# Expert matrix w2 loaded as two adjacent rows per partition instead of two rows 128 apart

## The chip, the cores and the metric

The kernel runs on one core of one Trainium2 chip, as a single launch. The metric is the device time in microseconds (us), read as the median over runs. Weights start in the chip's main memory (HBM) and reach the core's on-chip memory of 128 partitions (SBUF) by DMA; TensorE (PE) multiplies, and VectorE (DVE), ScalarE (ACT) and GpSimd (POOL) do the elementwise work. SyncE (SP) issues nearly all transfers here. Every core has 16 DMA engines, over which each transfer is spread.

## The reference

The program is one inference step of a hybrid decoder layer in float32: 256 prompt tokens and 8 sample tokens of width 1024 (and 16 meta tokens in front of the prompt) pass a normalisation, an input projection, a short convolution and a gated recurrence, an output projection, and then a mixture of 32 experts, 4 of which each token uses. The change lies in the experts:

```python
def _moe(x, router_w, router_b, w1, b1, w2, b2):
    logits = x.astype(jnp.float32) @ router_w.astype(jnp.float32) + router_b.astype(jnp.float32)
    top_logits, top_idx = lax.top_k(logits, TOP_K)
    gates = jax.nn.softmax(top_logits, axis=-1)
    combine = jnp.einsum('tk,tke->te', gates,
                         jax.nn.one_hot(top_idx, N_EXPERTS, dtype=jnp.float32)).astype(x.dtype)
    out = jnp.zeros_like(x)
    for e in range(N_EXPERTS):
        a = x @ w1[e] + b1[e]                      # w1[e]: 1024 x 2048
        glu = jnp.minimum(a[:, ::2], SWIGLU_LIMIT)
        lin = jnp.clip(a[:, 1::2], -SWIGLU_LIMIT, SWIGLU_LIMIT)
        act = glu * jax.nn.sigmoid(SWIGLU_ALPHA * glu) * (lin + 1)
        out = out + combine[:, e:e + 1] * (act @ w2[e] + b2[e])   # w2[e]: 1024 x 1024
    return out
```

All 32 experts' weights are read, 12 MiB each in float32, 384 MiB together.

## The kernel before

**Two parts.** The first 240 us or so hold the token mixers, the routing and the gathering of tokens. From there on the kernel runs over the experts in 16 pairs. The function `pair` on PE takes two experts at once: each expert has room for 64 tokens (`CAP`), and its two halves of the PE array compute expert 0 and expert 1 of the pair side by side.

**What one pair does on PE, in program order.** The bias (L1316); 128 matmuls with w1 (L1354), which walk over the 8 row tiles `t` of w1, for both experts; the gather of the next pair's tokens (L1307, 72 short matmuls); adding back the rows of the pair before (L1324, 6 products); three transposes of the gather matrix (L1373); eight transposes of the activations (L1381); and 64 matmuls with w2 (L1394), again over 8 row tiles. Between L1354 and L1381 DVE and ACT apply the gated activation into `lin`, a tile of 128 partitions (64 tokens of each expert) by 1024 columns, one column for each row of w2. A transpose of `lin` puts 128 of its columns on the partitions, ACT copies it from PSUM to `actT3` (L666), and `actT3[:, t]` is then the stationary operand of the products with row tile `t` of w2.

**The ring.** `ring` has 16 slots of one load each, 1 MiB (128 partitions of 8 KB). A pair needs 24 loads (`LOADS`): j = 0 to 15 are the row tiles of w1, alternating between the two experts, and j = 16 to 23 are w2, where one load holds two row tiles (`t` and `t + 1`) of one expert. SP issues the loads in this order with `load` (the first pair) and `load_pair` (the rest), w1 at L357 and w2 at L359. Before each load it waits for `w_used`, which PE raises when it has finished with a slot. PE in turn waits for a load's own semaphore (`landed`). So nothing but free slots and the transfers themselves set when a load starts, and the SP queue holds nothing but these loads in the expert stage.

**The views that say which rows go where.** One w1 load gives partition p a whole row of 2048 numbers, one run of 8 KB. One w2 load covers 256 rows of 1024 numbers; `w2_v` says that partition p takes row p and row 128 + p of them (`a` = 0 and 1), two runs of 4 KB that lie 512 KB apart in HBM:

```python
w1_v = expert_w1[0].rearrange("e (t p) n -> e t p n", p=P)
w2_v = expert_w2[0].rearrange("e (r a p) n -> e r p a n", a=2, p=P)
```

The rows that are multiplied together must be the same on both sides: with `w2_v` as above, row tile `t` is rows 128t to 128t + 127, and the transpose at L1381 reads columns 128t to 128t + 127 of `lin`.

Of the kernel before, what the change touches and what calls it, by code (L numbers as in the profile page):

```python
# [25 lines left out]
P = 128  # L26
# [31 lines left out]
def build_step(nc, x_prompt, x_sample, state_conv, state_rec, meta_tokens, norm_mix, w_in, conv_w,  # L58
# [4 lines left out]
    with ctx:  # L63
# [11 lines left out]
        def take(n):  # L75
            a = top[0]
            top[0] += n
            assert top[0] <= ARENA, top[0]
            return mem[:, a:a + n]


        ident = take(P)
# [32 lines left out]
        def from_(ap, n, at=0):  # L115

            return mem[:, ap.offset + at:ap.offset + at + n]
# [81 lines left out]
        glu, sig, lin = [from_(vtok, D, D * n) for n in range(3)]  # L199
# [91 lines left out]
        w_sb = {g: cut(slots(a), 512) for g, a in {FX: 6, IV: 14, QG: 10, OG: 0, BG: 2, HV: 4, CG: 6}.items()}  # L291
        wout_sb = [cut(slots(10), D), cut(slots(14), D)]
        w1_v = expert_w1[0].rearrange("e (t p) n -> e t p n", p=P)
        w2_v = expert_w2[0].rearrange("e (r a p) n -> e r p a n", a=2, p=P)

# [12 lines left out]
        def each_pair(eng, c, body, start=0):  # L310

            with eng.Fori(start, PAIRS // 2 - 1) as i:
                for k in range(2):
                    body(c, i, k, False)
            body(c, PAIRS // 2 - 1, 0, False)
            body(c, PAIRS // 2 - 1, 1, True)

        def num(c, i, k):
            return c * PAIRS + i * 2 + k

        def landed(eng, c, i, k, j):

            pos = LOADS * k + j
            slot = pos % SLOTS
            eng.wait_ge(ring_in[slot], (c * (PAIRS // 2) + i) * 48 + 16 * (pos // SLOTS) + 16)
            return slot

        @block.sync
        def _(sp):
# [70 lines left out]
            def first_loads(c):  # L400
                load_pair(c, 0, 1, False)
                each_pair(sp, c, load_pair, start=1)

            run_passes(sp, first_loads, lambda c: each_pair(sp, c, load_pair))
            for i in range(2):
                sp.wait_ge(fin_sb, i + 1)
# [129 lines left out]
        def _(act):  # L536
# [135 lines left out]
            def first_pass(c):  # L672
                act.wait_ge(parts_sb, 3)
                copy_xgT(0, 0)
                act.wait_ge(combT_ps, 1)
                act.activation(combT, ps[0:E, 5, 0:NT], ACT.Copy).then_inc(combT_sb, 1)
                each_pair(act, c, pair)
# [374 lines left out]
        def _(pe):  # L1052
# [10 lines left out]
            for i in range(3):  # L1063
# [4 lines left out]
                for t in range(KT):  # L1068
                    r, at = TILE_ROWS[i], TILE_COL[i]
# [63 lines left out]
            for what, a in SCHEDULE:  # L1133
# [40 lines left out]
                if what == "outer":  # L1174
                    h, n = a // 2, a % 2
# [109 lines left out]
            for i in range(3):  # L1285
                r = [P, P, NS][i]
# [13 lines left out]
            def gather(n, k):  # L1300

                pe.wait_ge(oh_sb, n + 1)
                for t in range(KT):
                    out = ps[:, 6 + t // 4, (t % 4) * P:(t % 4 + 1) * P]
                    for m in range(3):
                        for part in range(3):
                            last = mm(out, hn_hi_mid_lo[m][:, part, t * P:(t + 1) * P],  # L1307
                                      oh5[:, k, m].rearrange("p e s -> p (e s)"),
                                      start=(m == 0 and part == 0), stop=(m == 2 and part == 2))
                    if t % 4 == 3:  # L1310
                        last.then_inc(xgT_ps, 1)

            def bias(k):

                for b in range(4):
                    mm(ps[:, b, :], sel4[:, k].rearrange("p e s -> p (e s)"),  # L1316
                       b1_parts[0:96, b * 512:(b + 1) * 512], start=True, stop=False)
# [10 lines left out]
            def rows_of_y(n):  # L1328

                pe.wait_ge(y_sb, n)  # L1330
                for m in (2, 0, 1):
                    rows(m, ohgT, ysb)

            def rows_of_b2():

                pe.wait_ge(b2_in, 16)
                pe.wait_ge(combT_sb, 1)
                for m in (2, 0, 1):
                    rows(m, combT, b2_sb)

            def pair(c, i, k, last, adds="y"):

                n = num(c, i, k)
                if adds == "y":
                    pe.wait_ge(added, n * 3)
                if adds == "none":
                    pe.wait_ge(added, n * 3 + 3)
                bias(k)
                pe.wait_ge(xgT_sb, n * 2 + 2)
                for t in range(KT):  # L1350
                    slot = [landed(pe, c, i, k, 2 * t + e) for e in range(2)]
                    for b in range(4):
                        for e in range(2):
                            done = mm(ps[CAP * e:CAP * e + CAP, b, :], xgT4[:, k, t, CAP * e:CAP * e + CAP],  # L1354
                                      ring[:, slot[e], b * 512:(b + 1) * 512], start=False, stop=(t == KT - 1))
                            if b == 3:
                                done.then_inc(w_used, 1)
                        if t == KT - 1 and b == 1:
                            done.then_inc(a_ps, 1)
                if not last:  # L1360
                    gather(n + 1, 1 - k)

                pe.wait_ge(lin_sb, n * 2 + 2)
                if adds == "y":
                    rows_of_y(n)
                if adds == "b2":
                    rows_of_b2()
                pe.wait_ge(ohg_sb, n + 1)
                if adds == "none":
                    pe.wait_ge(y_sb, n)  # L1370
                for m in range(3):
                    r = [P, P, NS][m]
                    done = pe.transpose(ps[:, 4, m * P:m * P + r], ohg5[0:r, k, m].rearrange("p e s -> p (e s)"),  # L1373
                                        ident[0:r, 0:r])
                done.then_inc(ohgT_ps, 1)
                if not last:
                    pe.wait_ge(xgT_sb, n * 2 + 4)
                for half in range(2):
                    pe.wait_ge(act_sb, n * 2 + half + 1)
                    for q in range(4):  # L1380
                        done = pe.transpose(ps[:, 6 + half, q * P:(q + 1) * P],  # L1381
                                            lin[:, (4 * half + q) * P:(4 * half + q + 1) * P], ident)
                    done.then_inc(actT_ps, 1)
                pe.wait_ge(ohgT_sb, n + 1)
                pe.wait_ge(added, n * 3 + 1)
                for t in range(KT):
                    if t % 4 == 0:
                        pe.wait_ge(actT_sb, n * 2 + t // 4 + 1)
                    if t % 2 == 0:
                        slot = [landed(pe, c, i, k, 16 + t + e) for e in range(2)]  # L1390
                    for half in range(2):
                        for e in range(2):
                            col = (t % 2) * D + half * HALF
                            done = mm(ps[CAP * e:CAP * e + CAP, 4 + half, :], actT3[:, t, CAP * e:CAP * e + CAP],  # L1394
                                      ring[:, slot[e], col:col + HALF], start=(t == 0), stop=(t == KT - 1))
                            if t % 2 and half:
                                done.then_inc(w_used, 1)

            def first_pass(c):
                pe.wait_ge(b1_sb, 1)  # L1400
                pe.wait_ge(parts_sb, 3)
                pe.wait_ge(max_sb, 1)
                gather(0, 0)

                pe.wait_ge(comb_sb, 1)
                for i in range(3):
                    r = [P, P, NS][i]
                    last = pe.transpose(ps[0:E, 5, i * P:i * P + r], comb3[0:r, i], ident[0:r, 0:r])
                last.then_inc(combT_ps, 1)
                pair(c, 0, 0, False, adds="b2")  # L1410
                pair(c, 0, 1, False)
                each_pair(pe, c, pair, start=1)
                pe.wait_ge(added, PAIRS * 3)
                rows_of_y(PAIRS)
# [35 lines left out]
```

## Time and profile before

| | us |
|---|---|
| median of 3 runs | 1210.44 |
| lowest and highest | 1208.14, 1211.63 |
| the profiled execution | 1207.2 |
| its span, first to last instruction | 1205.5 |

The profile is that of one execution. Its span is 1.7 us shorter than that execution's own time and the execution is 3.2 us below the median. Times in the rows count from the start of the span. PE is busy 1073.1 us of the span, DVE 291.7, ACT 142.2 and POOL 75.3. A "releaser" is what ended an engine's wait by the record of semaphores. In the views of stretches, "DMA share" is the busy share of the 16 DMA engines; it can come out slightly above 1, since records of packets overlap. "LDWEIGHTS" (PEld) loads the stationary operand of a matmul and runs beside the matmul before it.

### The profile page before, as it was taken

The page shows a single profiled execution, that of the slowest core. Times are in us where ns is not written, and L with a number is a line of the kernel's source. Part 1 is how long each engine was busy: PE and PEld are TensorE (multiplying, and loading weights), DVE is VectorE, ACT ScalarE, POOL GpSimd, SP SyncE. Part 2 cuts the span into 40 slices and gives each one's busy share as a digit, 9 for nine tenths or more (in the row PEclk, how much of TensorE's full clock was granted, in tenths as well). Part 3 has the DMA queues.
Part 4 walks back from the last instruction along what each step waited for, and adds up shares of the span by engine and source line. Part 5 has one row for each costly group of instructions (what it writes and reads, how often), then busy time and mean ns, then how long its engine had stood idle before and what let it go on. Part 6 is the DMA issues. An engine that isn't in the chain of part 4 may idle for free.

```text
span 1205.5 us, 14443 instructions
## 1 busy us (share of the span) xinstructions
PE 1073.1 (89%) x5773; PEld 494.8 (41%) x5773; DVE 291.7 (24%) x466; ACT 142.2 (12%) x237; POOL 75.3 (6%) x114
## 2 busy tenths in 40 slices
PE   6999999499999988898989898989898989898984
PEld 3667784244434343434343434343434343434331
DVE  5348444503113030303030303030303030302022
ACT  3221112101011010101010101010101010101002
POOL 7016001600000000000000000000000000000000
PEclk9999999699999999999999999999999999999998
DMA  9851238169999999999999999999999999999991
GB/s 341 278 210 27 108 137 312 70 271 421 413 420 413 421 413 421 413 422 413 422 414 422 413 422 413 422 413 422 414 421 414 422 414 422 414 421 414 421 413 75
DMA packets 91671, 432.53 MB, mean 359 GB/s; under 512 B 7824, under 2 KB 16552, under 8 KB 58770
## 3 DMA queue, kind: packets, MB, share of 16 engines
q1 hardware_dynamic: 89504, 428.24, 87.8%
q0 software_dynamic: 864, 3.09, 0.8%
q10 hardware_dynamic: 1266, 0.70, 0.2%
q8 instruction: 25, 0.41, 0.1%
q14 instruction: 12, 0.10, 0.0%
HBM read 428.52 MB, written 3.48 MB: 358 GB/s over the span
## 4 chain that ended last, share of the span: by engine, by line
PE 55%; DMA 29%; SPq 9%; DVE 3%; issue 2%; ACT 1%; DVEq 0%; ACTq 0%
DMA ring<-in_expert_w 29%; PE ps L1394 13%; PE ps L1354 11%; SPq L357 9%; PE ps L1324 6%; PE ps L1307 6%; PE ps L1096 4%; PE ps L1080 4%; PE ps L1229 2%; PE ps L1381 1%; PE ps L1146 1%; PE ps L1162 1%; PE ps L1182 1%; PE ps L1373 1%; PE ps L1088 0%
## 5 line engine op out<-in xcount | busy, mean ns | idle before, releaser
L1354 PE MATMUL ps<-ring,mem 128*64 128x512 f32 x2048 | 457.3, 595 | 78.2 <-DMA ring<-in_expert_w 78.2
L1354 PEld LDWEIGHTS ps<-ring,mem 128*64 128x64 f32 x2048 | 153.2, 137 | 374.9 <-issue 374.8
L1394 PE MATMUL ps<-ring,mem 128*64 128x512 f32 x1024 | 224.1, 595 | 6.3 <-ACT mem L666 3.2
L997 DVE TENSOR_SCALAR mem<-ps 128x512 f32<-128x512 f32 x32 | 22.1, 692 | 735.2 <-PE ps L1354 735.2
L1394 PEld LDWEIGHTS ps<-ring,mem 128*64 128x64 f32 x1024 | 86.3, 137 | 134.1 <-issue 131.0
L659 ACT ACTIVATE mem<-mem 128x512 f32<-128x512 f32 x32 | 20.2, 630 | 526.5 <-DVE mem L997 526.5
L1324 PE MATMUL ps<-mem 128*128 128x512 f32 (+3 forms) x204 | 79.3, 601 | 2.6 <-DVE mem L999 1.4
L1307 PE MATMUL ps<-mem 128*128 128x128 bf16 x1152 | 68.5, 221 | 5.4 <-DVE mem L1019 5.4
L1307 PEld LDWEIGHTS ps<-mem 128*128 128x128 bf16 x1152 | 65.8, 99 | 17.6 <-issue 17.6
L1096 PE MATMUL ps<-mem,ring 128*128 128x280 f32 x256 | 62.9, 401 | 0.9 <-ACT mem L593 0.9
L1096 PEld LDWEIGHTS ps<-mem,ring 128*128 128x128 f32 x256 | 47.6, 190 | 13.4 <-issue 2.8
L979 DVE TENSOR_TENSOR mem<-mem,ps 128x1024 f32<-128x1024 f32 x34 | 41.4, 1221 | 16.4 <-PE ps L1324 16.4
L1324 PEld LDWEIGHTS ps<-mem 128*128 128x128 f32 (+3 forms) x204 | 26.2, 155 | 44.9 <-issue 41.1
L1080 PE MATMUL ps<-ring,mem 128*128 128x512 f32 x96 | 43.8, 616 | 0.4 <-ACT mem L562 0.4
L670 ACT ACTIVATE mem<-ps 128x1024 f32<-128x1024 f32 x16 | 16.4, 1024 | 220.3 <-PE ps L1394 220.3
L1080 PEld LDWEIGHTS ps<-ring,mem 128*128 128x128 f32 x96 | 18.9, 199 | 23.4 <-issue 22.8
L1229 PE MATMUL ps<-ring,mem 128*128 128x512 f32 x64 | 28.2, 596 | 0.0
L650 ACT ACTIVATE mem<-ps 128x512 f32<-128x512 f32 x32 | 19.1, 598 | 47.7 <-PE ps L1307 47.7
L999 DVE TENSOR_SCALAR mem<-ps 128x512 f32<-128x512 f32 x32 | 21.8, 680 | 0.0
L1010 DVE TENSOR_TENSOR mem<-mem 128x512 f32<-128x512 f32 x32 | 20.6, 684 | 0.0
L974 DVE TENSOR_TENSOR mem<-mem,ps 8x512 f32<-8x512 f32 x17 | 11.5, 675 | 37.6 <-PE ps L1324 37.6
L1004 DVE SCALAR_TENSOR_TENSOR mem<-mem 128x512 f32<-128x512 f32 x32 | 20.5, 683 | 0.0
(242 smaller groups left out, 564.4 us busy)
## 6 DMA issues: line engine op xcount, KB each, us to landing
ring<-in_expert_w SPq DMA_DIRECT2D x384, 1024.0 KB, 22.5
ring<-in_w_in SPq DMA_DIRECT2D x7, 2048.0 KB, 20.0
ring<-in_w_out SPq DMA_DIRECT2D x2, 2048.0 KB, 10.1
ring<-in_state_rec SPq DMA_DIRECT2D x4, 512.0 KB, 10.7
out<-ring SPq DMA_DIRECT2D x4, 512.0 KB, 12.0
ring<-in_x_prompt SPq DMA_DIRECT2D x2, 512.0 KB, 4.6
mem<-in_x_prompt POOLq DMA_DIRECT2D x2, 512.0 KB, 7.3
out<-mem SPq DMA_DIRECT2D x2, 512.0 KB
```

The lines of the kernel that those rows point to most:

```text
L357: sp.dma_start(ring[:, slot, :], w1_v[e, j // 2]).then_inc(ring_in[slot], 16)
L979: dve.tensor_tensor(h3[:, m], h3[:, m], ps[:, 2 * m:2 * m + 2, :].rearrange("p a n -> p (a n)"), ALU.add)\
L997: dve.tensor_scalar(glu[:, at], psA[:, half * D:(half + 1) * D:2], LIMIT, None, ALU.min)\
L999: dve.tensor_scalar(lin[:, at], psA[:, half * D + 1:(half + 1) * D:2], -LIMIT, LIMIT, ALU.max, ALU.min).then_inc(lin_sb, 1)
L1010: dve.tensor_tensor(lin[:, at], lin[:, at], sig[:, at], ALU.mult).then_inc(act_sb, 1)
L1080: last = mm(ps[:, bank, :], xT3[:, t, at:at + P], w_sb[g][:, t, :], start=(t == 0), stop=(t == KT - 1))
L1096: last = mm(ps[:, bank, 0:TOK], w_sb[g][:, t, j * P:(j + 1) * P], xT3[:, t, :], start=(t == 0), stop=(t == KT - 1))
L1229: last = mm(ps[:, (6, 4)[i] + n, :], yT3[:, k, TILE_COL[i]:TILE_COL[i] + P], wout_sb[k // 4][:, t, n * 512:(n + 1) * 512], start=(k == 0), ...
L1307: last = mm(out, hn_hi_mid_lo[m][:, part, t * P:(t + 1) * P], oh5[:, k, m].rearrange("p e s -> p (e s)"), start=(m == 0 and part == 0), st ...
L1324: last = mm(to, left[:, m * P:m * P + r], right[:, half * HALF:(half + 1) * HALF], start=True, stop=True)
L1354: done = mm(ps[CAP * e:CAP * e + CAP, b, :], xgT4[:, k, t, CAP * e:CAP * e + CAP], ring[:, slot[e], b * 512:(b + 1) * 512], start=False, s ...
L1394: done = mm(ps[CAP * e:CAP * e + CAP, 4 + half, :], actT3[:, t, CAP * e:CAP * e + CAP], ring[:, slot[e], col:col + HALF], start=(t == 0), ...
```

## The change

`w2_v` gives partition p of a w2 load the two adjacent rows 2p and 2p + 1 of its 256, which is one run of 8 KB. What was row tile `t` is now every second row of a block of 256, so the transpose for tile `t` reads every second column of the same 256 columns of `lin`, starting at column 0 for even `t` and at column 1 for odd `t`. The slots, the order of loads, the waits, the products and their number are the same, and the sum over the rows of w2 is taken in another order.

```diff
-        w2_v = expert_w2[0].rearrange("e (r a p) n -> e r p a n", a=2, p=P)
+        w2_v = expert_w2[0].rearrange("e (r p a) n -> e r p a n", a=2, p=P)
...
+        def act_cols(t):
+
+            return slice(t // 2 * 2 * P + t % 2, (t // 2 + 1) * 2 * P, 2)
...
                         done = pe.transpose(ps[:, 6 + half, q * P:(q + 1) * P],
-                                            lin[:, (4 * half + q) * P:(4 * half + q + 1) * P], ident)
+                                            lin[:, act_cols(4 * half + q)], ident)
```

No instruction moves. What the built program shows of it stands on SP, where the first two pairs' loads are issued. A row names the line, the operation, the destination and source, and the shape of one transfer. Before:

```order
L357 DMA ring<-in_expert_w1 128x2048 x8
L373 DMA out_5<-ring 128x8x128 x4
L375 DMA out_3<-mem 128x4x128
L359 DMA ring<-in_expert_w2 128x2x1024 x8
L357 DMA ring<-in_expert_w1 128x2048 x16
```

And after, where the lines have moved down by four in the file:

```order
L361 DMA ring<-in_expert_w1 128x2048 x8
L377 DMA out_5<-ring 128x8x128 x4
L379 DMA out_3<-mem 128x4x128
L363 DMA ring<-in_expert_w2 128x2048 x8
L361 DMA ring<-in_expert_w1 128x2048 x16
```

A w2 transfer had the shape 128 x 2 x 1024 (two runs for each partition) and has now the shape of a w1 transfer, 128 x 2048 (one run for each).

## Rows read from the trace of the kernel before

**Rows 1.** The page: busy time of each engine, and the DMA packets.
```profile
PE 1073.1 (89%) x5773; PEld 494.8 (41%) x5773; DVE 291.7 (24%) x466; ACT 142.2 (12%) x237; POOL 75.3 (6%) x114
...
DMA packets 91671, 432.53 MB, mean 359 GB/s; under 512 B 7824, under 2 KB 16552, under 8 KB 58770
```

**Rows 2.** PE's instructions of one pair: start, length, instruction, wait before it.
```profile
677.84 3.65 PE L1354 MATMUL ps<-ring,mem 128*64 128x512 f32 x16 [1.33 <-DMA ring<-in_expert_w]
...
690.51 1.09 PE L1381 MATMUL ps<-mem 128*128 128x128 f32 x8
691.90 13.95 PE L1394 MATMUL ps<-ring,mem 128*64 128x512 f32 x64 [0.30 <-issue]
...
706.75 10.52 PE L1354 MATMUL ps<-ring,mem 128*64 128x512 f32 x48
718.17 3.65 PE L1354 MATMUL ps<-ring,mem 128*64 128x512 f32 x16 [0.89 <-DMA ring<-in_expert_w]
...
738.06 2.37 PE L1354 MATMUL ps<-ring,mem 128*64 128x512 f32 x10 [1.34 <-DMA ring<-in_expert_w]
```

**Rows 3.** Waits over the span: who waited for whom, total us, times, longest.
```profile
PE ps L1354 <- DMA ring<-in_expert_w: 78.2, 64, 1.3
```

**Rows 4.** Busy time by stretch: length, PE, PEld, DVE, ACT, POOL, clock, DMA share, GB/s.
```profile
617.62:677.84 60.22, 53.76 (x292) 22.23 (x292) 9.94 (x15) 4.96 (x8) 0.00 (x0) 1.00 1.02 418
```

**Rows 5.** The same view, of stretches in which w2 loads arrive.
```profile
252.00:270.00 18.00, 18.00 (x86) 6.03 (x84) 0.00 (x0) 0.00 (x0) 0.00 (x0) 1.00 1.02 412
619.00:635.00 16.00, 15.46 (x123) 8.76 (x121) 9.94 (x15) 3.94 (x7) 0.00 (x0) 1.00 1.03 411
680.00:696.00 16.00, 15.70 (x123) 8.96 (x121) 9.83 (x15) 3.93 (x7) 0.00 (x0) 1.00 1.03 411
```

**Rows 6.** The same view, of stretches in which w1 loads arrive.
```profile
641.00:677.00 36.00, 30.92 (x140) 10.42 (x136) 0.00 (x0) 1.02 (x1) 0.00 (x0) 1.00 1.01 421
702.00:737.00 35.00, 29.89 (x134) 9.94 (x130) 0.00 (x0) 2.31 (x2) 0.00 (x0) 1.00 1.01 421
```

**Rows 7.** DMA packets of 252 to 268 us, w2 arriving; q1 is SP's queue: packets, MB, share.
```profile
DMA packets 1712, 6.62 MB, mean 414 GB/s; under 512 B 96, under 2 KB 96, under 8 KB 1712
...
q1 hardware_dynamic: 1712, 6.62, 102.6%
```

**Rows 8.** DMA packets of 641 to 677 us, w1 arriving.
```profile
DMA packets 2173, 15.15 MB, mean 421 GB/s; under 512 B 236, under 2 KB 236, under 8 KB 411
...
q1 hardware_dynamic: 2173, 15.15, 101.3%
```

**Rows 9.** The eight transposes a pair: duration in ns min/median/max, first and last start.
```profile
L1381 PEld LDWEIGHTS ps<-mem x128: 138/140/231, 282.9 to 1170.8; 128*128 128x128 f32 x128
L1381 PE MATMUL ps<-mem x128: 272/273/421, 282.9 to 1170.9; 128*128 128x128 f32 x128
```

**Rows 10.** The chain that ended last, from the last pair's w1 on.
```profile
1132.59 27.32 DMA ring<-in_expert_w
...
1160.05 3.67 PE ps L1354 x16
...
1171.55 13.97 PE ps L1394 x64
...
1201.87 1.27 DVE mem L1048
```

**Rows 11.** PE's instructions around the first pair's w2.
```profile
246.08 27.69 PE L1354 MATMUL ps<-ring,mem 128*64 128x512 f32 x128
...
284.80 14.83 PE L1394 MATMUL ps<-ring,mem 128*64 128x512 f32 x64
```

**Rows 12.** Busy time by stretch, as in rows 4, around the same place and at the end.
```profile
250.00:270.00 20.00, 20.00 (x96) 6.75 (x94) 0.00 (x0) 0.00 (x0) 0.00 (x0) 1.00 0.97 381
288.00:294.00 6.00, 6.00 (x32) 2.14 (x29) 0.00 (x0) 0.00 (x0) 0.00 (x0) 1.00 1.01 421
1175.00:1180.00 5.00, 5.00 (x26) 2.07 (x24) 0.00 (x0) 0.00 (x0) 0.00 (x0) 1.00 0.62 252
```

## The prediction

> **What bounds the kernel now.** I read the busy times first. PE is busy for 1073.1 of 1205.5 us [rows 1], which looks like a kernel bound by PE, but an average over stages says little, so I went on to one pair of experts. From 617.62 to 677.84, 60.22 us, PE is busy for 53.76 us and idle for 6.46 us, while the 16 DMA engines are at a share of 1.02 and move 418 GB/s [rows 4]. PE's own instructions show which side waits: near the end of a pair's w1, each group of 16 matmuls of L1354 (3.65 us, two loads' worth) begins after a wait of about 0.9 to 1.3 us that a DMA ends [rows 2]. Over the span there are 64 such waits, 78.2 us [rows 3]. So in the steady expert stage the transfers set the pace and PE follows. The chain that ended last says the same for the end: the last pair's last w1 matmuls start at 1160.05, when a load lands, and everything behind them runs off PE, ACT and DVE until 1205.5, 45.4 us later [rows 10].
>
> **How fast each kind of load arrives.** In a pair, the starts at 718.17 and 738.06 are both set by a landing, and four steps of two w1 loads lie between them (64 of the pair's 128 matmuls: 48 stand before 718.17 and 16 after 738.06): 19.89 / 4 = 4.97 us a step, 2.486 us for a w1 load of 1 MiB [rows 2]. Sixteen of them take 39.78 us. The pair takes 738.06 - 677.84 = 60.22 us [rows 2, 4], so its eight w2 loads, also of 1 MiB each, take 60.22 - 39.78 = 20.44 us, 2.555 us each. The stretches agree: w1 arrives at 421 GB/s [rows 6] and w2 at 411 or 412 GB/s [rows 5], which makes 2.491 and about 2.55 us a load (1,048,576 bytes over the rate).
>
> **What the change does to w2's loads.** In 252 to 268 us, 1,616 packets of 4 KB and 96 small ones took 102.6% of 16 engines for 16 us, 262.7 us of engine time, about 0.162 us for a 4 KB packet if the small ones take about 0.01 us (an assumption; at zero it is 0.1626) [rows 7]. In 641 to 677 us, 175 packets of 4 KB, 1,762 of 8 KB and 236 small ones took 583.5 us, which leaves about 0.314 us for an 8 KB packet [rows 8]. Two 4 KB packets thus cost 0.324 us against 0.314 for one of 8 KB. After the change a w2 transfer has the shape of a w1 transfer, its 256 packets become 128, its bytes lie in one contiguous MiB of HBM as before, and it lands in the same slots. I take w1's rate for it, the nearest row there is: 2.555 - 2.486 = 0.069 us less for each load. By the three readings the saving for one load is 0.060 us (rates), 0.069 us (landings) or 128 x 0.010 / 16 = 0.082 us (packets, whose records overlap more at 4 KB, with the share at 1.026 against 1.013, so that this one overstates). I use the landings, since PE waits for those.
>
> **How many loads count.** All 128 w2 loads are issued in the saturated stretch, but the last pair's eight are off the path: the DMA engines go quiet within 1175 to 1180 (share 0.62) [rows 12], while PE takes 1171.55 to 1185.5 for their 64 matmuls without a wait between them [rows 10]. What is ahead of the last w1 landing at 1160 counts: 15 pairs x 8 = 120 loads. 120 x 0.069 = **8.3 us**. At 0.060 it is 7.2 us, at 0.082 9.8 us.
>
> **Is the stream unbroken?** It must be, or a faster w2 only lengthens a gap. It starts near 250 and stands at a share of 1.02 [rows 5, 12]. The tightest place is the first pair. PE frees all 16 slots by the end of its w1 at 273.8 [rows 11], then none until two row tiles of L1394 are through, some 3.5 us after 284.80, at 288.3. The DMA engines need 8 x 2.555 + 8 x 2.486 = 40.3 us for those 16 slots, until about 290.5, a cover of 2.2 us, and there is no dip in 288 to 294 (share 1.01) [rows 12]. After the change the cover is 0.55 us shorter. If SP needs more than the 1.6 us left to get the next load going, at most those 0.55 us are lost. I take nothing for it and keep 0 to 0.55 us for the range. Later pairs have more cover, since PE, which needs 53.8 us for a pair, gains on a stream that needs 60.
>
> **The transposes.** Eight a pair, 128 in all, now read the stationary operand with a step of two numbers. They take 1.09 us a pair, 0.137 us each, the length of their LDWEIGHTS (0.140 us) [rows 2, 9]. The trace of before has no weight load with a step. From below I take 0, since a step can't make the read shorter than the dense one; from above I take a doubling, 1.1 us a pair, for a read that fetches twice the bytes for the same numbers. In 15 pairs either end is hidden, by PE's 6.46 us of idle time (5.9 us after the change). If that cover were gone, the upper end would be 15 x 1.1 = 16.5 us. In the last pair the transposes lie on the chain [rows 10], so 0 to 1.1 us are exposed. I take 0, as it is the same count of columns, and keep 1.1 us for the range. The page "SBUF — State Buffer" of the Trainium skill (section on the DMA port swizzle) says that reads run at full bandwidth with two hits in each line of 16 bytes, which would allow up to four float32; a step of two has exactly two hits in a line, and no row here shows it. By it the exposed cost is 0.
>
> **The sum.** The profiled execution took 1207.2 us; less 8.3 it is 1198.9. It was 3.2 us below the median of 1210.44, so for the median I predict 1210.44 - 8.3 = 1202.1 us.
>
> **Rivals.** (A) *The packet's length is not why w2 is slower.* In most pairs w2 arrives while DVE and ACT work on the activations and PE does its short matmuls and transposes: in 619 to 635 DVE is busy for 9.94 us, in 641 to 677 not at all [rows 5, 6]. If that work slowed the transfers into SBUF, 8 KB packets would arrive no faster at that place, the gain would be about 0, and the time 1210.4. Against it stands the first pair, where w2 arrives during L1354's matmuls with DVE and ACT at 0.00: still 412 GB/s [rows 5]. That leaves perhaps 1 of the 10 GB/s to the other work. A mild form is that an 8 KB packet saves something but less than w1's rows say, some 3 us, time 1207. The Trainium skill's page "DMA: Bandwidth & Descriptors" ("Why small descriptors are slow") has a fixed cost of about 3 cycles a packet and holds that joining descriptors pays only up to 256 B; the same page's 850 MHz makes that 3.5 ns a packet, by which the estimate is 120 x 128 x 3.5 ns / 16 = 3.4 us and the time 1207.0. The trace disagrees with it in size, since two 4 KB packets are about 10 ns longer than one of 8 KB [rows 7, 8]. Chance of A, both forms: 0.11.
> (B) *The stepped transposes make PE the bound, and it ends slower.* PE has 6.46 us of idle time a pair; above it each microsecond shows. Eight transposes share it, so the point is 0.81 us more for each, on top of 0.14, nearly seven times as long. At 1.1 us each (0.96 more, 7.7 us a pair) a pair would take 53.76 + 7.7 = 61.5 us, 1.2 us more than now, 15 x 1.2 = 18 us slower and 7.7 us more in the last pair: 1236. For it speaks only that no row shows such a read; against it, that the number of columns is the same. Chance 0.02.
> (C) *The change does not do what it says*: the transfer is still cut at 4 KB. Then the time stays at 1210.4. Against it: a w1 transfer has the very same shape and shows 8 KB packets [rows 8]. Chance 0.02.
>
> **How the numbers follow.** Forecast (w2 at w1's rate, 7 to 10 us gained) 0.85, A 0.11, B 0.02, C 0.02. The bounds of the forecast are 1210.44 - 9.8 = 1200.6 and 1210.44 - 7.2 + 0.55 + 1.1 = 1204.9; the median of three runs that lie 1208.1 to 1211.6 apart adds some 2 us at both ends, to 1198.6 and 1206.9, which takes in A's mild form at 1207. I give 1198.5 to 1207. About 0.3%, 3.6 us, is what a measurement of this kernel can tell from no change. Faster by more than that: 0.85 and a little of A's mild form, 0.86. Same: the rest of A and C, 0.12. Slower: B, 0.02.
>
> **What the profile after should show.** Packets fall by 128 x 128 = 16,384, to about 75,290, and those under 8 KB by 32,768, to about 26,000. Stretches with w2 arriving read about 421 GB/s with a share near 1.01. A pair takes 60.22 - 0.55 = 59.7 us. PE's waits on L1354 fall from 78.2 us by about the gain, to some 70. The eight transposes stay at 1.1 us. The last w1 group starts near 1151.8, and the 45.4 us behind it stay. **What would make it wrong:** w2's stretches still at 411 GB/s with 8 KB packets (A), still 58,770 packets under 8 KB (C), transposes of about 1 us each (B), or a DMA share below 1 near 290.

## The result and the profile after

The changed kernel took 1199.22 us in the median of its first 4 runs (1196.11 to 1200.17), against 1209.29 us for the kernel before in 4 runs (1207.96 to 1211.63). The medians lie 10.1 us apart. The ratio of the two kernels' runs is 0.991, with a 95% interval of 0.9885 to 0.9936, which is 7.7 to 13.9 us. Two repeats, further down, gave 8.1 and 8.6 us. The forecast was 8.3 us and 1202.1, with a range of 1198.5 to 1207.

The profiled execution of the changed kernel took 1196.11 us with a span of 1194.3. Its page of the profile has the packets that the new shape promised:

```profile
span 1194.3 us, 14443 instructions
...
PE 1072.3 (90%) x5773; PEld 496.3 (42%) x5773; DVE 291.3 (24%) x466; ACT 142.0 (12%) x237; POOL 75.3 (6%) x114
...
DMA packets 75287, 432.53 MB, mean 362 GB/s; under 512 B 7824, under 2 KB 16552, under 8 KB 26002
```

Against [rows 1], there are 16,384 packets fewer and 32,768 fewer of those under 8 KB, and the same bytes. PE does the same work. The waits on loads answer to [rows 3]: 9.7 us less, in 57 waits instead of 64.

```profile
PE ps L1358 <- DMA ring<-in_expert_w: 68.5, 57, 1.4
```

The stretches answer to [rows 5, 6] (length, busy time of PE, PEld, DVE, ACT, POOL, clock, DMA share, GB/s). In the first, second and fourth w2 arrives, in the third w1:

```profile
252.00:270.00 18.00, 18.00 (x86) 6.03 (x84) 0.19 (x1) 0.00 (x0) 0.00 (x0) 1.00 1.01 425
616.00:634.00 18.00, 17.50 (x126) 9.62 (x124) 8.15 (x13) 3.30 (x6) 0.00 (x0) 1.00 1.01 421
642.00:674.00 32.00, 26.74 (x122) 9.12 (x120) 0.54 (x1) 0.00 (x0) 0.00 (x0) 1.00 1.01 422
676.00:692.00 16.00, 15.75 (x111) 8.68 (x109) 7.77 (x12) 3.14 (x6) 0.00 (x0) 1.00 1.01 422
```

The 10 GB/s between the two matrices have gone, also where DVE and ACT are busy. PE's instructions of one pair (start, length, instruction, wait) answer to [rows 2]:

```profile
611.79 3.65 PE L1358 MATMUL ps<-ring,mem 128*64 128x512 f32 x16 [1.32 <-DMA ring<-in_expert_w]
...
624.47 1.22 PE L1385 MATMUL ps<-mem 128*128 128x128 f32 x8
626.19 13.95 PE L1398 MATMUL ps<-ring,mem 128*64 128x512 f32 x64 [0.50 <-ACT mem L670]
...
671.41 3.65 PE L1358 MATMUL ps<-ring,mem 128*64 128x512 f32 x16 [1.31 <-DMA ring<-in_expert_w]
```

A pair now takes 671.41 - 611.79 = 59.62 us, 0.60 less than 60.22. The transposes (L1385) take 1.22 us instead of 1.09.

**Where the time went.** The span splits into what stands ahead of the experts' first w1 matmul, the stage from there to the last w1 landing, and the tail. For the changed kernel, and then for the kernel before:

```profile
243.79:1148.86 905.07, 831.34 (x4479) 342.78 (x4478) 148.01 (x222) 83.10 (x127) 0.59 (x1) 1.00 1.01 419
1148.86:1194.30 45.44, 28.47 (x115) 11.21 (x115) 17.29 (x24) 9.78 (x17) 0.00 (x0) 0.90 0.46 186
```

```profile
246.08:1160.05 913.97, 829.89 (x4479) 340.38 (x4478) 147.97 (x222) 83.17 (x127) 0.59 (x1) 1.00 1.01 415
```

The loaded stage is 8.90 us shorter, and the tail stays (45.44 and 45.45 us). The remaining 2.3 us of the 11.2 us between the two spans lie ahead of 246 us, where the change has no instruction: the first 32 matmuls of the input projection took 13.97 us in this execution and 15.89 in that of before.

```profile
16.21 13.97 PE L1084 MATMUL ps<-ring,mem 128*128 128x512 f32 x32 [0.69 <-ACT mem L566]
```

```profile
16.48 15.89 PE L1080 MATMUL ps<-ring,mem 128*128 128x512 f32 x32 [0.38 <-ACT mem L562]
```

Both lengths turn up with either kind of w2 load in the runs below: 13.97 us with the old loads (the run with w1 in runs of 4 KB), 15.80 with the new ones (the run with the loads alone). So by these runs it is a difference between executions and not the change; its cause stays open.

### The profile page after: what moved, and what is told of

Read it like the earlier page. It is cut to its first block, busy times and chain, and to the rows that moved or that the text cites. A ratio compares the mean times of both kernels' runs of the same rounds, so it can differ in the third digit from the quotient of the medians.

```text
span 1194.3 us, 14443 instructions
## 1 busy us (share of the span) xinstructions
PE 1072.3 (90%) x5773; PEld 496.3 (42%) x5773; DVE 291.3 (24%) x466; ACT 142.0 (12%) x237; POOL 75.3 (6%) x114
## 4 chain that ended last, share of the span: by engine, by line
PE 55%; DMA 30%; SPq 9%; DVE 3%; issue 2%; ACT 1%; ACTq 0%; DVEq 0%
DMA ring<-in_expert_w 29%; PE ps L1398 13%; PE ps L1358 11%; SPq L361 9%; PE ps L1328 7%; PE ps L1311 6%; PE ps L1100 4%; PE ps L1084 3%; PE ps L1233 2%; PE ps L1385 1%; PE ps L1150 1%; PE ps L1166 1%; PE ps L1186 1%; PE ps L1377 1%; PE ps L1092 0%
## 5 line engine op out<-in xcount | busy, mean ns | idle before, releaser
L674 ACT ACTIVATE mem<-ps 128x1024 f32<-128x1024 f32 x16 | 16.4, 1024 | 220.2 <-PE ps L1398 220.2
## 6 DMA issues: line engine op xcount, KB each, us to landing
ring<-in_w_out SPq DMA_DIRECT2D x2, 2048.0 KB, 10.1
```

## The experiments

The theory is that a load's rate is set by the length of its contiguous runs, and that 120 w2 loads count. (A run is here a stretch of adjacent bytes that goes to one partition.) The rival was that w2 arrived more slowly because of what else went on meanwhile. Beside the medians I use the length of the expert stage, from the first w1 matmul to the end of the span, since the part ahead of it varies between executions of any kernel. It is 1205.5 - 246.08 = 959.4 us in the profile of before and 1194.3 - 243.79 = 950.5 after.

### The change again, and its two halves

The first run repeats the changed kernel.

> The changed kernel itself, repeated in five rounds, to narrow the interval. The forecast's sum (120 loads at 0.069 us) puts it 8.3 us below the kernel before, ratio 0.993. The first measurement had 10.1 us and 0.991. If the term for one load was simply too small, the repeat stays near 10 us; if the extra 2 us were drift between runs, it comes back to 8 to 9 us.

Measured: 1200.21 us against 1208.27, ratio 0.9932 (0.9909 to 0.9955), 8.1 us. In its profile the experts start at 248.02, 4.2 us later than in the first profile of the same kernel, and the stage up to the last w1 landing takes 906.25 us, 7.7 us less than before:

```profile
16.71 15.63 PE L1084 MATMUL ps<-ring,mem 128*128 128x512 f32 x32 [0.38 <-ACT mem L566]
...
240.17 6.63 PE L1311 MATMUL ps<-mem 128*128 128x128 bf16 x72 [5.38 <-DVE mem L1023]
...
248.02:1154.27 906.25, 832.85 (x4479) 343.32 (x4478) 148.00 (x222) 83.14 (x127) 0.59 (x1) 1.00 1.01 419
```

So the profiled execution of the first comparison owes 2.3 of its 11.2 us to the part ahead of the experts. That the 10.1 us between the medians had the same source is likely but not shown, since the other executions have no profile. The experts' stage varies too: in this second profile the stream began thinly, with 329 GB/s in 253 to 260 us against 392 at the same distance from the stage's start in the first, which is about 1 of the 1.2 us between 906.25 and 905.07. The third measurement gives this stage once more.

> The changed kernel once more, beside the last two on the same chip: 8 us below the kernel before (7 to 10), the number that they are compared with.

Measured: 1200.36 us against 1208.91, ratio 0.9924 (0.9905 to 0.9943), 8.6 us; the expert stage took 1197.8 - 247.04 = 950.8 us. The three profiles of the changed kernel thus have 950.5, 951.7 and 950.8 us, 7.7 to 8.9 less than the kernel before.

The next kernel has the new loads and the old transposes:

```diff
-                                            lin[:, act_cols(4 * half + q)], ident)
+                                            lin[:, (4 * half + q) * P:(4 * half + q + 1) * P], ident)
```

> The changed w2 loads with the transposes reading dense columns as before, so that activations are multiplied with the wrong rows of w2 (that part of the result is changed, the work is the same). My theory: the loads are the whole gain and the stepped transposes cost only what is exposed in the last pair, so this is within 0.2 us of the changed kernel. The rival that the stepped transposes cost something in every pair: 15 x 0.13 us, about 2 us faster than the changed kernel.

Measured: 1200.57 us, ratio 0.993 (0.9908 to 0.9951), the same as the changed kernel beside it. The other half, on the changed kernel's text:

```diff
-        w2_v = expert_w2[0].rearrange("e (r p a) n -> e r p a n", a=2, p=P)
+        w2_v = expert_w2[0].rearrange("e (r a p) n -> e r p a n", a=2, p=P)
```

> The kernel before with stepped transposes alone, the w2 loads as before, so that activations are multiplied with the wrong rows of w2 (that part of the result is changed, the work is the same). My theory: the eight transposes of a pair take 1.22 us instead of 1.09, hidden but for the last pair, so 0 to 0.3 us slower than the kernel before. The rival that they are exposed in every pair: 2 us slower.

Measured: 1208.26 us against 1208.27, ratio 0.9997 (0.9984 to 1.0011). The stepped transposes alone (minimum, median, maximum in ns, and the same of the kernel with dense ones and new loads) show that they do cost PE something:

```profile
L1385 PEld LDWEIGHTS ps<-mem x128: 195/209/226, 282.9 to 1170.7; 128*128 128x128 f32 x128
```

```profile
L1385 PEld LDWEIGHTS ps<-mem x128: 138/140/230, 286.5 to 1165.4; 128*128 128x128 f32 x128
```

A weight load takes 0.209 us instead of 0.140, and the eight transposes 0.13 us more in all. In every pair but the last, PE's idle time hides it. Within the intervals the whole gain is the loads'.

### The dose: other run lengths

If the length of a run sets the rate, w1 must slow down in the same way when it is cut like the old w2:

```diff
-        w1_v = expert_w1[0].rearrange("e (t p) n -> e t p n", p=P)
+        w1_v = expert_w1[0].rearrange("e k (h n) -> e (k h) n", h=2).rearrange("e (t a p) n -> e t p a n", a=2, p=P)
...
-                    sp.dma_start(ring[:, slot, :], w1_v[e, j // 2]).then_inc(ring_in[slot], 16)
+                    sp.dma_start(cut(ring[:, slot, :], D), w1_v[e, j // 2]).then_inc(ring_in[slot], 16)
```

> The kernel before with the w1 loads cut into two runs of 4 KB for each partition, 512 KB apart, as its w2 loads are; the rows of w1 land in other partitions, so the experts' first product is changed and the work is the same. My theory, that the length of a run sets the rate of a load: w1's 240 loads in the saturated stage take 2.555 instead of 2.486 us each, 16.6 us slower than the kernel before (14 to 20), and the stretches with w1 arriving read 411 GB/s. The rival that w2's stretches were slower because of what DVE, ACT and PE did meanwhile: no change, and those stretches stay at 421 GB/s.

Measured: 1226.01 us against 1208.27, ratio 1.0156 (1.0131 to 1.018), 17.7 us slower. PE's waits in w1 now end every 5.12 us, 2.560 us a load instead of 2.486, and a stretch with w1 arriving and DVE idle reads 410 GB/s:

```profile
668.73 3.65 PE L1354 MATMUL ps<-ring,mem 128*64 128x512 f32 x16 [1.47 <-DMA ring<-in_expert_w]
673.85 3.65 PE L1354 MATMUL ps<-ring,mem 128*64 128x512 f32 x16 [1.47 <-DMA ring<-in_expert_w]
...
640.00:674.00 34.00, 29.79 (x138) 10.55 (x136) 0.00 (x0) 1.03 (x1) 0.00 (x0) 1.00 1.03 410
```

240 loads x 0.074 = 17.8 us, and the expert stage became 1221.0 - 243.92 = 977.1 us, 17.7 longer. This takes rival A away: the same cut costs the same, whatever DVE and ACT do. Then w2 in runs of 2 KB:

```diff
-        w2_v = expert_w2[0].rearrange("e (r a p) n -> e r p a n", a=2, p=P)
+        w2_v = expert_w2[0].rearrange("e k (h n) -> e (k h) n", h=2).rearrange("e (r a p) n -> e r p a n", a=4, p=P)
...
-                    sp.dma_start(cut(ring[:, slot, :], D), w2_v[e, (j - 16) // 2]).then_inc(ring_in[slot], 16)
+                    sp.dma_start(cut(ring[:, slot, :], HALF), w2_v[e, (j - 16) // 2]).then_inc(ring_in[slot], 16)
```

> The kernel before with each w2 load cut into four runs of 2 KB for each partition (half rows, which lie 256 KB apart), so that the rows of w2 land in other places and the experts' second product is changed; the work is the same. My theory, a fixed cost for each run: one load took 2.555 us with 256 runs and 2.486 with 128, which is 0.0086 us for each run on each engine (0.069 x 16 / 128). With 512 runs a load takes 2.69 us, so 120 x 0.138 = 16.6 us slower than the kernel before (12 to 20). The rival, a cost that sets in only past some length: much less than that, or much more.

Measured: 1227.18 us against 1208.91, ratio 1.0151 (1.0126 to 1.0176), 18.3 us slower. The last w1 group starts at 627.17 in one pair and at 688.62 in the next:

```profile
627.17 3.65 PE L1354 MATMUL ps<-ring,mem 128*64 128x512 f32 x16 [1.33 <-DMA ring<-in_expert_w]
...
688.62 3.65 PE L1354 MATMUL ps<-ring,mem 128*64 128x512 f32 x16 [1.32 <-DMA ring<-in_expert_w]
```

That is a period of 61.45 us; less 39.78 for w1, a w2 load takes 2.709 us. And in the other direction, runs of 16 KB for w2, which take two slots, so that four adjacent rows go to a partition:

```diff
-        w2_v = expert_w2[0].rearrange("e (r p a) n -> e r p a n", a=2, p=P)
+        w2_v = expert_w2[0].rearrange("e (r p a) n -> e r p a n", a=4, p=P)
...
-            return slice(t // 2 * 2 * P + t % 2, (t // 2 + 1) * 2 * P, 2)
+            return slice(t // 4 * 4 * P + t % 4, (t // 4 + 1) * 4 * P, 4)
...
+                    two = ring[:, slot:slot + 2, :].rearrange("p a n -> p (a n)")
+                    sp.dma_start(cut(two, D), w2_v[e, (j - 16) // 4]).then_inc(ring_in[slot], 16)
```

> The changed kernel with four adjacent rows of w2 for each partition, one run of 16 KB over two slots, four w2 loads of 2 MiB a pair; transposes read every fourth column. If the fixed cost for a run goes on past 8 KB, half the runs save another 4 x 0.0086 = 0.034 us for each MiB, 120 x 0.034 = 4 us below the changed kernel, some 12 us below the kernel before. The rival, that a run is cut at 8 KB or that 8 KB is already at the engines' rate: the same time as the changed kernel.

Measured: 1196.62 us against 1208.91, ratio 0.9901 (0.9881 to 0.992), 12.3 us below the kernel before and 3.7 below the changed kernel beside it. A period is 730.91 - 671.55 = 59.36 us:

```profile
671.55 3.65 PE L1369 MATMUL ps<-ring,mem 128*64 128x512 f32 x16 [1.30 <-DMA ring<-in_expert_w]
...
730.91 3.65 PE L1369 MATMUL ps<-ring,mem 128*64 128x512 f32 x16 [1.33 <-DMA ring<-in_expert_w]
```

Less 39.78 for w1, that is 19.58 / 8 = 2.448 us for each MiB of w2. The rate is what the theory gives, but the 3.7 us between the medians are in part luck. The profiled execution's expert stage is 1194.1 - 244.50 = 949.6 us, only 0.9 to 2.1 less than the changed kernel's. Fifteen periods would give 15 x (59.62 - 59.36) = 3.9 us. Two things take most of it back: SP waits for four used slots before it refills any that held w2, and the stream runs thin at the first pair, by (1.01 - 0.75) x 6 = 1.6 us; and the tail is 1194.1 - 1147.40 = 46.7 us, 1.3 longer, as PE now waits for a load of 2 MiB in the last pair's w2 (0.87 us).

```profile
288.00:294.00 6.00, 6.00 (x30) 2.19 (x28) 0.00 (x0) 0.00 (x0) 0.00 (x0) 1.00 0.75 279
```

The control keeps these transfers of 2 MiB, slots and waits, but with two runs of 8 KB for each partition (`"e (r b p a) n -> e r p b (a n)", b=2, a=2`):

> The control for the 16 KB run: w2 in the same four transfers of 2 MiB a pair over two slots each, but with two runs of 8 KB for each partition; waits and slots as with 16 KB, transposes as in the changed kernel. My theory that the length of a run decides and not the size of a transfer: w2 at 2.486 us a MiB, the changed kernel's time (8.5 us below the kernel before), some 3.7 us above the kernel with runs of 16 KB. The rival that the larger transfer was what saved: the 16 KB kernel's time, 12 us below the kernel before.

Measured: 1203.22 us against 1207.8, ratio 0.9953 (0.9936 to 0.997), 4.6 us. The stretch with w2 arriving has 422 GB/s and a period is 737.19 - 677.56 = 59.63 us, both the changed kernel's, so the size of a transfer gives nothing. Nor does the distance between a partition's runs, which is 1 MiB in HBM here. The expert stage, 1203.0 - 247.66 = 955.3 us, is some 4 us longer than the changed kernel's, and most of that lies in one place. SP has the waits of the run before, and at the first pair the stream runs dry:

```profile
288.00:294.00 6.00, 6.00 (x28) 2.15 (x28) 0.02 (x1) 0.68 (x2) 0.00 (x0) 0.90 1.01 416
294.00:300.00 6.00, 6.00 (x32) 2.18 (x30) 0.00 (x0) 0.00 (x0) 0.00 (x0) 1.00 0.52 191
...
676.00:692.00 16.00, 14.43 (x115) 8.50 (x115) 9.45 (x15) 3.83 (x7) 0.00 (x0) 1.00 1.01 422
```

A share of 0.52 for 1.01 over 6 us is a loss of 2.9 us; the tail, 46.8 us, has the other 1.4. The loss is larger than the 1.6 us of the run before with the same waits. In this execution PE began the first pair's w2 products 40.6 us into the stage and there 38.5 us, so the slots came free later. The changed kernel, which waits slot by slot, has 416 GB/s and a share of 1.01 in 294 to 300, and its second execution, where PE began them after 40.5 us, has 426 and 1.02. So its cover was enough.

### A version that beats both

All expert loads in runs of 16 KB. With two adjacent rows of w1 for each partition too, the gather must deliver every second column of the tokens for one row tile. In the first try GpSimd wrote its three bf16 parts in that order.

> As the last one, with the w1 loads too in runs of 16 KB over two slots (two adjacent rows for each partition); GpSimd writes the gathered operand's columns in the matching order. With the same fixed cost for a run, 360 MiB save 0.034 us each, 12 us below the changed kernel and some 20 below the kernel before, less what GpSimd's stepped writes cost ahead of the first pair (0 to 5 us). The rival: no gain over the changed kernel, and a loss of what those writes cost.

Measured: 1220.65 us, ratio 1.0093 (1.0072 to 1.0113), 11.7 us slower. The expert stage itself is short, 1220.1 - 274.83 = 945.3 us, but starts 29 us late. GpSimd's first operations of this step, here and then with the reads stepped in place of the writes:

```profile
215.21 4.73 POOL L534 CAST mem<-mem 8x1024 bf16<-8x1024 f32 x1 [26.37 <-PE ps L1237]
220.02 2.81 POOL L536 TENSOR_TENSOR mem<-mem 8x1024 f32<-8x1024 f32 x1
```

```profile
212.55 1.11 POOL L534 CAST mem<-mem 8x1024 bf16<-8x1024 f32 x1 [26.37 <-PE ps L1237]
213.74 2.10 POOL L536 TENSOR_TENSOR mem<-mem 8x1024 f32<-8x1024 f32 x1
```

> All expert loads in runs of 16 KB, where the first try held the expert stage back by some 28 us, since GpSimd wrote the parts of the gathered operand in single steps of 256 bytes (4.7 us for one operation, 1.0 to 2.1 before). Here GpSimd writes densely and reads in steps of two numbers. If that is near the old pace (up to 1 us more for each of 12 operations), the 13.5 us that the rate gives over the changed kernel show: 18 to 22 us below the kernel before. The rival that a stepped read is as slow as the stepped write: 12 us above the kernel before, as in the first try.

Measured: 1193.05 us against 1207.8, ratio 0.989 (0.9868 to 0.9911); by the medians 14.8 us, by the ratio 13.3. The stage takes 1190.3 - 245.62 = 944.7 us, and two w1 groups of four slots begin 9.79 us apart, 2.448 us a MiB:

```profile
670.98 7.09 PE L1362 MATMUL ps<-ring,mem 128*64 128x512 f32 x32 [2.72 <-DMA ring<-in_expert_w]
...
719.91 8.78 PE L1362 MATMUL ps<-ring,mem 128*64 128x512 f32 x32 [2.54 <-DMA ring<-in_expert_w]
729.70 7.09 PE L1362 MATMUL ps<-ring,mem 128*64 128x512 f32 x32 [1.00 <-DMA ring<-in_expert_w]
```

The group at 719.91 took 8.78 us for 7.09, at a mean granted clock of 0.81; the wait after it is shorter by as much, so it cost nothing.

The same with GpSimd untouched and the gather's products reading stepped columns:

> All expert loads in runs of 16 KB, with GpSimd as in the kernel before and the gather's 72 products a pair reading their bf16 stationary operand in steps of two. The f32 transposes' weight loads took 0.209 us for 0.140 with a step. If the gather's grow by the same half, 0.05 us each, a pair gets 3.6 us longer on PE, 57.5 of the 58.7 us that the transfers need, still hidden but for the first gather: 16 to 21 us below the kernel before. The rival that they grow by more than 0.07 us each: PE becomes the bound, and the gain shrinks or turns into a loss.

Measured: 1193.5 us, ratio 0.988 (0.9862 to 0.9897), stage 945.9 us. The 3.6 us a pair that were feared for PE did not come: the 72 products took 4.20 us a pair, against 4.19 with dense columns.

The last run takes the version with stepped reads and refills the first two slots of four after three uses, where that version waits for four:

```diff
-                    sp.wait_ge(w_used, n * LOADS + j // 4 * 4 - SLOTS + 4)
+                    sp.wait_ge(w_used, n * LOADS + j // 4 * 4 - SLOTS + (4 if j % 4 else 3))
```

> The kernel with all expert loads in runs of 16 KB and GpSimd's stepped reads, where SP waited for four used slots before it refilled the first two of them. Here the first two are refilled after three uses, which is when both are free. The stream then starts about 1.7 us earlier at the first pair, and the dip at 294 to 300 us (371 for 426 GB/s) shrinks. Expected: 1 to 2 us below the former version, 15 to 17 us below the kernel before. The rival, that this gap is not on the path: no change, 14 us below.

Measured: 1196.0 us, ratio 0.9888 (0.987 to 0.9907), stage 1194.8 - 249.84 = 945.0 us. The 1 to 2 us did not come, and the edit turned out to change nothing that a clock sees. SP's first issue in the stage follows PE's first w1 matmul by 256.95 - 249.84 = 7.11 us, and by 252.78 - 245.62 = 7.16 us in the version without the edit: PE works on both experts side by side, so it gives back the third and fourth slot one matmul apart. Whether an earlier refill would help stays untested.

```profile
256.95 7.67 SPq L365 DMA_DIRECT2D ring<-in_expert_w  x4
```

```profile
252.78 7.67 SPq L365 DMA_DIRECT2D ring<-in_expert_w  x4
```

The three versions with 16 KB everywhere can't be told apart. They lie 12 to 15 us below the kernel before, where 15 to 22 had been expected. The rate alone would give 15 x (60.22 - 58.72) = 22.5 us, by a pair's period of 58.72 (670.98 to 729.70), and the stage became only 959.4 - 944.7 = 14.7 us shorter. By the trace, two things account for 6.9 of the missing 7.8 us, and a third for most of the rest. The stream starts 7.16 us into the stage, and in the changed kernel 247.47 - 243.79 = 3.68 us, since a load of two slots must wait for two row tiles. And the last landing releases 32 matmuls (7.09 us) in place of 16 (3.65 us), so that the tail is 1190.3 - 1141.41 = 48.9 us instead of 45.4. At the first pair the stream is thin for 6 us, 371 GB/s against 426 behind it, about 0.8 us:

```profile
1141.41 7.09 PE L1362 MATMUL ps<-ring,mem 128*64 128x512 f32 x32 [1.51 <-DMA ring<-in_expert_w]
```

```profile
294.00:300.00 6.00, 6.00 (x30) 2.17 (x28) 0.00 (x0) 0.00 (x0) 0.00 (x0) 1.00 0.95 371
```

## Why the prediction came out as it did

**What bounds the kernel.** Right. The share stayed above 1 through the expert stage, the waits on loads fell by 9.7 us, about what the loads gained, and taking w1's or w2's rate away made the kernel slower by the forecast's own arithmetic (17.7 us for 240 loads at 0.074, 18.3 for 120 at 0.154).

**The rate of the new loads.** Right in kind, too small in size. The forecast gave w2 the rate of w1, 0.069 us less for each load. The period of 59.62 us less 39.78 for w1 leaves 19.84 / 8 = 2.480 us a load, 0.075 less than 2.555. The forecast for a pair was 59.7. The dose in w1 gives 0.074. So this term was some 7% too small: it stood in the sum with 120 x 0.069 = 8.3 us, and 120 x 0.074 = 8.9 us, the 8.90 us of the first profile.

**How many loads count.** Right. The last pair's eight gave nothing; the tail of 45.4 us did not move.

**The stream at the first pair.** Right: no dip with 8 KB. That the place is tight was right as well, since a coarser wait of SP made the stream thin or dry there in two runs.

**The transposes.** The direction of the cost was open and 0 was taken. They cost 0.13 us a pair, of which only the last pair's can show. The Trainium skill's page "SBUF — State Buffer" (section on the DMA port swizzle) allows a step of two float32 at full rate. The weight loads went from 0.140 to 0.209 us, so the measurement disagrees for TensorE's stationary operand.

**The sum: the step that failed.** The forecast was 8.3 us and the first comparison had 10.1. The mechanism held; two terms of the sum were off. One is the price of a load, 0.069 us where the runs have 0.074 to 0.075, which is 0.6 us in all. The larger one was put at nothing: the sum takes the profile's own 3.2 us to the median as all there is to the difference between executions, and so leaves the part ahead of the experts equal on both sides. In the two profiled executions it was 2.3 us shorter after. Three executions of the changed kernel begin the experts at 243.79, 247.04 and 248.02 us, and why is open. With the interval of 7.7 to 13.9 us, the first comparison alone can't tell 10.1 from 8.3.

The repeats came to 8.1 and 8.6 us, and the expert stage was 7.7 to 8.9 us shorter. That the repeats lie so near 8.3 is partly luck: by the price of a load they should have had 8.9, and the profiled execution of the first repeat lost about 1 us at the start of its stream.

**Rival A** (something other than the length) fell with the first dose. Its mild form, some 3 us, was too small. The estimate of 3.4 us by the fixed cost for a packet in the Trainium skill, page "DMA: Bandwidth & Descriptors" ("Why small descriptors are slow"), was too small as well, because a run costs more here, as the section below shows. **Rival B** needed 0.81 us more for each transpose, and there were 0.02. **Rival C** fell with the packet count.

## What to carry to other kernels

Where a stream of loads keeps the DMA engines full, count the contiguous runs: each costs its engine a fixed time, so read both matrices' rates off the trace and give the slower one the shape of the faster. Rows of a contraction can be dealt to partitions in any order as long as the other operand is read with the same step, and what the step costs an engine with idle time is hidden (here 0.13 us a pair on PE). Before a gain from the stream is counted, find the place where the stream is refilled last: a coarser wait there cost 1.6 and 2.9 us where some 9 to 12 were to be gained, and larger loads throughout gave back a third of their gain, most of it at the two ends of the stream. And compare the stage that the change touches, beside the medians: one of the gains here stood in the medians with 3.7 us and in the stage with 0.9 to 2.1.

## What the runs showed of the hardware

A MiB into 128 partitions over 16 engines took 2.709 us in runs of 2 KB (32 runs for each engine), 2.555 to 2.560 in runs of 4 KB (16), 2.480 to 2.486 at 8 KB (8) and 2.448 at 16 KB (4). The steps are 0.15, 0.07 and 0.04 us for 16, 8 and 4 runs fewer, so by these differences each run costs its engine 8 to 10 ns beside its bytes, from 2 to 16 KB. The fixed cost of about 3 cycles for a packet in the Trainium skill, page "DMA: Bandwidth & Descriptors" ("Why small descriptors are slow"), which is an estimated 3.5 ns at its 850 MHz, is under half of it. What that section says of joining descriptors is about packing several into one packet; here the runs themselves became longer, so no run tests it. Twice the transfer size with the same runs changed nothing (422 GB/s).

TensorE's weight load of 128 x 128 float32 took 0.209 us with a step of two and with a step of four (the run with w2 at 16 KB), against 0.140 dense; eight transposes in a row took 1.22 to 1.23 us against 1.09. The gather's bf16 weight load took 0.098 us, dense and with a step of two.

GpSimd took 4.7 us for a cast to bf16 that wrote in steps of 256 bytes, against 1.1 us when it wrote densely and read float32 in steps of two.
